# S5 stage: poles turned amid a token tile, six homes for the input tables, stores ahead of loads; last combine: three tiles summed by TensorE

## What is computed

```
A_bar = exp(dt * A);  B_bar = ((A_bar - 1) / A) * B
step: states = scan(A_bar, B_bar u, s);  y = Re(C states)
y = y + d * u
z = gelu(y) @ w_out;  val, gate = split(z);  mix = val * sigmoid(gate)
...
x = layer_norm(ALPHA * x + sum over e of combine[:, e] * (h_e @ w_down[e]))
```

## Time and profile before

| | us |
|---|---|
| median of three runs (1462.12 to 1470.71) | 1466.73 |
| profiled execution | 1460.83 |
| its span, first to last instruction | 1459.3 |
| PE busy / DVE busy / ACT busy in it | 1231.9 / 1005.2 / 708.5 |

### The profile page before, as it was taken

How to read it: one execution, slowest core, us unless ns; L and a number is a source line. 1 busy time by engine, 2 the same in 40 slices (tenths; PEclk the granted TensorE clock), 3 DMA queues, 4 the chain that set the end, 5 groups by cost and what they waited for, 6 DMA issues and landing times.

```text
span 1459.3 us, 17295 instructions
## 1 busy us (share of the span) xinstructions
PE 1231.9 (84%) x6797; PEld 959.3 (66%) x6797; DVE 1005.2 (69%) x1067; ACT 708.5 (49%) x634; POOL 126.0 (9%) x189
## 2 busy tenths in 40 slices
PE   6899998798899999997493834989988999999960
PEld 5898888585466776665372724967854777777740
DVE  5884756445568888787778896342465688888848
ACT  4652332113377777766122813631353777777730
POOL 2000000000400000000300110000004000000021
PEclk9998998598999999999697876999989999999985
DMA  9542010233599999998535053350035999999945
GB/s 266 211 106 74 5 62 6 76 140 116 187 343 383 392 385 382 380 377 298 131 58 102 1 48 19 117 203 31 28 115 196 351 396 396 397 395 380 396 152 148
DMA packets 78929, 301.02 MB, mean 206 GB/s; under 512 B 22965, under 2 KB 40753, under 8 KB 66513
## 3 DMA queue, kind: packets, MB, share of 16 engines
q1 hardware_dynamic: 63128, 246.07, 47.6%
q0 software_dynamic: 15744, 54.18, 11.9%
HBM read 264.23 MB, written 33.64 MB: 204 GB/s over the span
## 4 chain that ended last, share of the span: by engine, by line
PE 57%; DVE 20%; DMA 12%; ACT 6%; issue 3%; SPq 2%; POOL 1%; DVEq 0%; ACTq 0%; POOLq 0%
PE ps L2349 15%; PE ps L2351 14%; PE ps L2350 14%; DMA raw<-in_moe_w_down 7%; DVE wlo L722 4%; ACT whi L629 3%; PE ps L787 2%; DMA u_d<-ub 2%; PE ps L1753 2%; DMA raw<-in_w_in_ab 1%; PE ps L812 1%; PE ps L1751 1%; PE ps L2462 1%; DVE hf L2244 1%; PE ps L2460 1%
## 5 line engine op out<-in xcount | busy, mean ns | idle before, releaser
L722 DVE TENSOR_TENSOR wlo<-raw,whi 128x4096 fp32r<-128x4096 f32 x92 | 406.6, 4422 | 123.6 <-ACT whi L629 123.5
L629 ACT ACTIVATE whi<-raw 128x4096 fp32r<-128x4096 f32 x92 | 333.6, 3628 | 98.4 <-DMA raw<-in_moe_w_down 89.3
L2349 PE MATMUL ps<-whi,xet_lo 128*96 128x512 f32 x528 | 212.6, 403 | 11.4 <-issue 11.2
L2351 PE MATMUL ps<-whi,xet_hi 128*96 128x512 f32 x528 | 208.8, 395 | 0.0
L2350 PE MATMUL ps<-wlo,xet_hi 128*96 128x512 f32 x528 | 208.5, 395 | 0.0
L2349 PE MATMUL ps<-ft_hi,wlo 128*128 128x288 f32 x384 | 120.1, 313 | 3.6 <-DVE wlo L2094 3.6
L2349 PEld LDWEIGHTS ps<-whi,xet_lo 128*96 128x96 f32 x528 | 87.0, 165 | 51.7 <-issue 18.5
L2350 PE MATMUL ps<-ft_lo,whi 128*128 128x288 f32 x384 | 117.1, 305 | 0.0
L2351 PE MATMUL ps<-ft_hi,whi 128*128 128x288 f32 x384 | 116.6, 304 | 0.0
L2351 PEld LDWEIGHTS ps<-whi,xet_hi 128*96 128x96 f32 x528 | 85.7, 162 | 36.8 <-issue 0.2
L2350 PEld LDWEIGHTS ps<-wlo,xet_hi 128*96 128x96 f32 x528 | 86.0, 163 | 34.4 <-issue 1.1
(11 more groups left out here) (455 smaller groups left out, 2110.4 us busy)
## 6 DMA issues: line engine op xcount, KB each, us to landing
raw<-in_moe_w_gate SPq DMA_DIRECT2D x32, 2048.0 KB, 9.6
raw<-in_moe_w_up SPq DMA_DIRECT2D x32, 2048.0 KB, 9.3
raw<-in_moe_w_down SPq DMA_DIRECT2D x32, 2048.0 KB, 9.6
yg<-ysb POOLq DMA_DIRECT2D x32, 384.0 KB, 6.0
xe<-xg POOLq DMA_DIRECT2D x28, 384.0 KB, 8.1
raw<-in_w_in_ab SPq DMA_DIRECT2D x16, 512.0 KB, 6.4
raw<-in_w_out_s SPq DMA_DIRECT2D x4, 2048.0 KB, 8.8
xg<-zeros POOLq DMA_DIRECT2D x4, 1536.0 KB, 14.7
```

What stands on the lines that cost most here:

```text
L629: sa.activation(whi[q][:], raw[q][:], ACT.Copy).then_inc(s(f"hi{q}" + L), 1)
L722: v.tensor_tensor(wlo[q][:], raw[q][:], whi[q][:].bitcast(F32), ALU.subtract).then_inc(s(f"lo{q}" + L), 1)
L2349: te.matmul(out, l_lo, r_hi, start=first, stop=False)
L2351: return te.matmul(out, l_hi, r_hi, start=False, stop=last)
```

## The change

1. `poles_turned`: the seven transposes of the pole tables move from the head of tile 4 to between the two halves of tile 3. ACT's copy to `t4` moves ahead of the copies of tiles 3 and 4.
2. SP's order: the store of tile 0 goes ahead of the loads of B and C, the store of tile 1 and the load of tile 0 between the real and the imaginary part of these, and from then on the store of tile i goes ahead of the load of tile i - 1.
3. Six homes for `wt`: two new ones at `Z_AT`, where the pole tables were. Turns 0 and 1 are made before the wait for the last tile, 2 to 5 after it, 6 and 7 reuse homes 2 and 3 and come after five output turns. `pr` moves to another address and is filled earlier.
4. The output turns run in the order 0, 2, 4, 6, 1, 3, 5, 7, 8, and PE waits for each by its place in it.
5. Last combine, tiles 2 to 4: ACT writes the gates on the diagonals of `dgate`, PE adds `ident` times `xtok` and `dgate` times the two gathered tiles in PSUM, and DVE takes the statistics and the first step of the norm from there.

```diff
+            def u_store(i):
+            def u_load(i):
...
+            u_store(0)
+            sp_.wait_ge(s("ln_x"), 2 * NT)
+            b_and_c(0, "re")
+            u_store(1)
+            u_load(0)
+            b_and_c(1, "im")
+            for i in range(2, NT):
+                u_store(i)
+                u_load(i - 1)
+            u_load(NT - 1)
...
-        wt = [at(f"s5_wt{i}", [P, QT, CL, GC], SPAD_AT + 4 * QT * P * i) for i in range(4)]
+        wt = [at(f"s5_wt{i}", [P, QT, CL, GC], Z_AT + 4 * QT * P * i if i < 2 else SPAD_AT + 4 * QT * P * (i - 2))
+              for i in range(6)]
+        wt += wt[2:4]
...
+        W_PARTS = ((0, 2), (2, 6), (6, 8))
+        O_ORDER = (0, 2, 4, 6, 1, 3, 5, 7, 8)
...
             u_out(2)
+            act.wait_ge(s("s5_pt"), 1)
+            sa.activation(t4[:].rearrange("p a b -> p (a b)"), ps[:, 4, 0:4 * PAIRS], ACT.Copy).then_inc(s("s5a"), 1)
             u_out(3)
+            u_out(4)
             act.wait_ge(s("s5_pt"), 2)
...
+                if t >= 6:
+                    dve.wait_ge(s("s5_fill"), 16 + 2 * (t - 4) + 2)
...
+            w_turns(*W_PARTS[0])
             dve.wait_ge(s("y"), 2 * NT)
...
+            w_turns(*W_PARTS[1])
             dve.wait_ge(s("u72"), 16 * NT)
...
+            o_turns(0, 5)
+            w_turns(*W_PARTS[2])
+            o_turns(5, O_TURNS)
...
+                    if half and poles:
+                        poles_turned()
...
+        def sums_act(act):
+            act.wait_ge(s("routed"), 2)
+            for i in range(SUMMED, NT):
+                n = TILES[i][1]
+                for k in range(2):
+                    ins = nc.scalar.activation(dgate[0:n, i - SUMMED, k, 0:n], ident[0:n, 0:n], ACT.Copy,
+                                               scale=gate[0:n, k, i:i + 1])
+            ins.then_inc(s("x_alpha"), 1)
+        def sums_pe(pe):
+            te = nc.tensor
+            pe.wait_ge(s("x_alpha"), 5)
+            pe.wait_ge(s("got0"), 32 * 3)
+            for i in range(SUMMED, NT):
+                n = TILES[i][1]
+                for half in range(2):
+                    te.matmul(sum_banks(i)[:, half, :], ident[0:n, 0:n], xtok[0:n, i, 512 * half:512 * half + 512],
+                              start=True, stop=False)
+            for i in range(SUMMED, NT):
+                n = TILES[i][1]
+                pe.wait_ge(s(f"got{i % 4}"), 32 * (2 + 2 * (i // 4)))
+                for half in range(2):
+                    for k in range(2):
+                        ins = te.matmul(sum_banks(i)[:, half, :], dgate[0:n, i - SUMMED, k, 0:n],
+                                        ygat[i % 4][k][0:n, 512 * half:512 * half + 512], start=False, stop=(k == 1))
+                ins.then_inc(s("y"), 1)
...
+                if l == 1 and i >= SUMMED:
+                    dve.wait_ge(s("y"), 4 * NT + i - SUMMED + 1)
+                    ln_stats(dve, link, "ffn1", i, sum_banks(i))
+                    ln_norm(dve, link, "ffn1", i, sum_banks(i))
+                    continue
```

More of the change, by code:

```diff
@@ L1075, in s5_sp, with b_and_c @@
                 sp_.dma_start(dst, src).then_inc(s("s5_par"), 16)
[L1076 to L1077 removed]
+            def b_and_c(ri, nm):
                 b_src = a[f"s5_b_{nm}"][0].rearrange("(a b) p c -> (b p) a c", b=2)
@@ L1131, in w_done @@
         def w_done(t):
-            return 12 * (t // 4) + (5, 8, 11, 12)[t % 4]
+            first, last = [part for part in W_PARTS if part[0] <= t < part[1]][0]
+            return 3 * first + (3 * (t - first) + 5 if t < last - 1 else 3 * (last - first))
+        W_PARTS = ((0, 2), (2, 6), (6, 8))
         W_ALL = w_done(7)
         Z_STEPS = NC_P >> LEVELS
+        O_ORDER = (0, 2, 4, 6, 1, 3, 5, 7, 8)
         O_TURNS = 9
@@ L1492, in w_sum, with w_turns @@
             def w_sum(t):
-                dve.wait_ge(s("w_m"), w_done(t) - 3 + (t % 4 == 3) * 2)
-                tt(wt[t % 4][:], wt[t % 4][:], w_tmp[t % 2][:].rearrange("p (a s c) -> p a s c", a=QT, c=GC),
+                dve.wait_ge(s("w_m"), 3 * t + 2)
+                tt(wt[t][:], wt[t][:], w_tmp[t % 2][:].rearrange("p (a s c) -> p a s c", a=QT, c=GC),
                    S_ if t % 2 == 0 else A_).then_inc(s("w_m"), 1)
-            def w_turns(t0, t1, first, last):
-                for t in range(t0, t1):
+            def w_turns(first, last):
+                for t in range(first, last):
                     w_products(t)
@@ L1501, in w_turns @@
                         w_sum(t - 1)
-                if t1 == last:
-                    w_sum(last - 1)
-            w_turns(0, 4, 0, 4)
+                w_sum(last - 1)
+            w_turns(*W_PARTS[0])
+            dve.wait_ge(s("y"), 2 * NT)
+            v.tensor_copy(pf[:], pw[:, :, 0:CL, :])
+            for r_ in range(2):
+                v.tensor_copy(poles[0][:, r_, r_, :], pw[:, 0, CL, :])
+            ts(poles[0][:, 0, 1, :], pw[:, 1, CL, :], -1.0, None, M)
+            v.tensor_copy(poles[0][:, 1, 0, :], pw[:, 1, CL, :]).then_inc(s("bbar"), 1)
+            w_turns(*W_PARTS[1])
             dve.wait_ge(s("u72"), 16 * NT)
@@ L1637, in x_transpose, with token_major @@
                         ins.then_inc(s("xt"), 1)
-            def token_major(i, j, slots, first_chunk, between=None, route=False):
+            def token_major(i, j, slots, first_chunk, between=None, route=False, poles=False):
                 t0, n = TILES[i]
@@ L1672, in s5_pe @@
                 pe.wait_ge(s("x_split"), NT + i + 1)
-                token_major(i, i, (1, 0), 0, 2 * i + 1 if i < 2 else None)
+                token_major(i, i, (1, 0), 0, 2 * i + 1 if i < 2 else None, poles=i == NT - 2)
                 if i < 2:
```

108 lines of the change are left out of this document (55 added, 53 removed).

## The result

The changed kernel takes 1444.9 us (median of 4 runs, 1436.8 to 1450.4) where the kernel before takes 1467.1 us in the runs beside it; the ratio is 0.9851 with a 95% interval of 0.9825 to 0.9878. The forecast was 1444.8 us.

What follows compares the result with a forecast made beforehand. It took SP's store-load DMA chain, with DVE waits beside it, to bound the S5 stage, and DVE the last combine. Gains of 14.0 and 7.9 us, 21.9 in all, from 1466.73 gave 1444.8 us; range 1437 to 1455.

Steps and rivals of the forecast that it cites:

- The powers: S5 stage: with the poles turned amid tile 3, DVE starts the pole powers at 762.0, 8.5 us earlier.
- Stores and loads: S5 stage: SP's new order lands u at 789.7 to 792, before DVE wants it at 795.9; the 1.38 us wait goes.
- cover 4 to 6 us: S5 stage: margin for B and C imaginary, queued behind load 0 on SP, to land before needed; cost nothing.
- rival (e): S5 stage: load 0 and store 1 delay the C loads, DVE and PE wait, kernel slower (1473 at worst landing); chance 0.03.
- Homes and order: S5 stage: DVE's 4.36 us wait for home 0 goes, output tables end at 836.9, not 851.0; stage total 14.0 us.
- The K chain: S5 stage: K starts between 831.3 and 834.7, its 2.94 us wait goes, spreads issue at 850 to 854.3, hidden.
- (b): K chain takes over: PE's clock falls waiting for input turn 6 and stays low into K; 1449 to 1453; chance 0.16.
- 2 to 7: S5 stage: us by which the spreads, landing at 876 to 881, precede the states wanted at 883.1.
- The last combine: Tail: gated sums of tiles 2 to 4 leave DVE, 2.63 us a tile, 7.9 us; PE ahead with 2 us cover.
- Reading PSUM: Last combine: DVE reading PSUM instead of SBUF put at 0, between -0.06 and +0.2 us an instruction.
- The sum and the medians: Whole kernel: 14.0 + 7.9 = 21.9 us, subtracted from the median 1466.73 gives 1444.8; the expert phases shift as a whole.
- rival (a): S5 stage: u comes late, loads landing at 795 to 798, ACT's copies to 801.2; 2.9 us lost, 1447.7; chance 0.10.

Runs made afterwards that it cites:

- e3: Changed kernel with the pole transposes back at the head of the last tile and ACT's copy of them behind the fourth u copy; 1450.5 us, ratio 0.9905.
- e9: Changed kernel with both the poles turned late and SP's old order, keeping six homes, order of turns and new combine; 1455.5 us, ratio 0.9916.
- e4: Changed kernel with SP's old order (B and C ahead of all stores, each load behind its own store); 1447.3 us, ratio 0.9875.
- e10: The changed kernel run once more, without edits; 1448.9 us, ratio 0.9867.
- e5: Changed kernel with the input turns in four homes again, on the weights' slots; 1455.7 us, ratio 0.9911.
- e8: Changed kernel with four tiles summed by TensorE and the identity products ahead of the wait for tile 0's rows; 1447.8 us, ratio 0.9859.
- e11: As e8, with the identity products of tiles 1 to 3 made twice to keep TensorE busy; 1445.0 us, ratio 0.9842.
- e12: Changed kernel, three tiles summed, with the identity products ahead of the wait for tile 0's rows; 1447.3 us, ratio 0.9858.
- after: The changed kernel with all parts of the change, first run; 1444.9 us, ratio 0.9851 to the kernel before.
- e1: Changed kernel with the last combine put back (DVE sums all five tiles), so the S5 part alone; 1452.5 us, ratio 0.9906.
- e7: Changed kernel with four tiles summed by TensorE instead of three; 1450.6 us, ratio 0.9890.
- e6: Changed kernel with the output turns in natural order 0 to 8; 1443.1 us, ratio 0.9816.
- e2: Kernel before with the last combine alone changed (three tiles summed by TensorE); 1458.5 us, ratio 0.9954.
- before: The kernel without the change; 1467.1 us in the runs beside the changed kernel.

## Why the prediction was right

The time, 1444.8, was met, and by its own steps; where a step was off, something next to it absorbed it. That the median came within 0.1 us is luck: the same kernel's second median is 4.0 us higher, and its single executions lie up to 19 us apart. What was right beyond luck is the gain in the traces, 22.05 us for 21.9. Counted from the anchor, predicted times are those of the text less 740.99.

**The powers.** Predicted 8.5 us earlier, measured 8.65 (20.86 for 21.0); the transposes start at 764.18 - 744.29 = 19.89 where 760.9 - 740.99 = 19.9 was read from the middle of tile 3. The attribution was too simple: the 8.5 us were put down to part 1 alone. They are 2.74 by SP's order and then 5.91 by the poles (29.51, 26.77 in e3, 20.86), or in the other order 6.95 by the poles and 1.67 by SP's (29.48 in e9, 22.53 in e4, 20.86).

**Stores and loads.** Here a term was mis-sized. "B and C imaginary to 759" and "cover 4 to 6 us": behind store 1 and load 0 their issue ended at 769.03, 765.7 on the clock of before, and took 11.81 us for eight where 6.93 was taken over from the earlier trace rows. The cover was not 4 us but nothing: in the second trace of the changed kernel (e10) TensorE waits 0.56 us for the last of them in front of its transposes, in e5 to e8, e11 and e12, with the same order there, 0.28 to 0.74 (in after itself and in e1 not at all). ACT's copy of tile 4 comes 38.60 us after the anchor in after and 39.19 in e7, against 38.16 in the kernel before. The tables end at 95.82 to 95.85 in all of these but e5, so it cost nothing. TensorE in e10:

```profile
771.64 1.09 PE L1743 MATMUL ps<-ident,s_craw 128*128 128x128 f32 x8 [0.56 <-DMA s_craw<-in_s_c_im]
```

So rival (e) was nearer than its 0.03 says: with store 1 and load 0 ahead the issue took 5 us longer, and it did push tile 4, by up to 1 us; u had that much to spare. u landed when ACT started its sorting copies, 795.97 - 744.29 = 51.68, which is 792.7 on the clock of before; "789.7 to 792" was 0.7 us short. That it came out free is due to the 795.9 for DVE, which held to 0.2 us (799.06, less 3.30: 795.76).

**Homes and order.** The waits of 4.36 and 1.38 us are gone, output tables predicted at 836.9 and measured at 836.83; 14.0 predicted, 14.17 measured. What the step did not see is the larger half of what the homes do: the wait for the weights' slots that the earlier powers would otherwise have met (5.43 us in e5). The prediction let DVE run from the powers to the sorting copies "without a wait" and was right only because the new homes lie elsewhere.

**The K chain.** Predicted start 831.3 to 834.7, measured 832.24 (835.54 less 3.30); the clock did fall at the wait for input turn 6 (2.12 us where (b) had 3.5), as (b) feared, to 0.57, but was back for K. That it was back is no rule: in e10, the same kernel, K began at 0.50, and in e1, the same S5 stage, it took 17.08 us. The 29 us of (b), all of K at half clock, came in no trace, and the padding of the states stands at 137.36 to 137.44 in all three. Spreads' issue predicted 850 to 854.3, measured 851.55. The DMA engines are busy with them to the window that ends at 882 (its share, 0.96 of 1.5 to 1.7 just before, puts the end near 881.3, 878.0 on the clock of before; 876 to 881 predicted), and the first output product starts at 886.30 behind the padded states, so the cover is some 5 us, inside the "2 to 7". The natural order of output turns makes no difference (e6), where the wait for DVE is gone too; that the order "was made for" the chain was reading a purpose into it.

**The last combine.** 7.9 predicted, 7.88 measured. Inside it, the price of a product was half of what it is: a float32 product shows as two records in the trace (six products are 12 records, a tile's four are 8), and the 0.44 us of the earlier trace rows is that of one record. "Six take 5.3 us at most" is the price at 1.00; they took 7.99 us, since TensorE starts at 0.50 and is back at 1.00 only in the window from 1422. A tile's four take 3.69 us where "1.8 to 3.5" was written. It cost nothing, since the rows came late too (tile 2's at 1424.70). The cover at the last tile is 1.3 us (sums end 1436.81, wanted 1438.09), not 2, and it is thinnest at tile 3: half of the 7.13 us for two tiles puts its sum at 1433.2 (an estimate), wanted at 1433.93.

**Reading PSUM.** The statistics and the first step cost the same from either place (0.69, 0.68, 1.28 us), so the 0 us taken from the earlier trace rows stands. By the Trainium skill's "VectorE: DVE Perf Modes", section on the TRN2 errata, a source in PSUM has 62 cycles more; the nine instructions would have taken 0.6 us more, an estimate from that figure. The trace doesn't agree: none of these instructions is longer from PSUM by more than 0.01 us.

**The sum and the medians.** 21.9 predicted, 22.05 in the landmarks; and "the expert phases shift as a whole" was right in kind, since in no experiment does their length follow the edits, though the pair of profiles alone would have said 13.5 us.

**Two slips without effect.** Of the "five store-load rounds of about 7.4 us" in the earlier trace rows the first takes 3.8 us and only the others 7.4. In rival (a) a landing at 795 to 798 gives copies that end at 798.7 to 801.7, not at 801.2.

## What to carry to other kernels

Where two profiles differ in stretches that nobody edited, count from the nearest untouched instruction ahead of the edit: that gave 0.03 us of agreement here where medians of one kernel differed by 4. The price of a removed wait is what comes next in the engine's list, so edits that remove one wait each are not a sum of parts (the same new buffers were worth 5.5 us alone and 9.5 together with an earlier start). Before work is pulled forward into TensorE's idle time, look at what TensorE does at the end of that time: having finished early it started the critical product at half clock (e8, e12). With three tiles that cost more than finishing late (tail 26.98 us in e12, 26.15 in after). With four it cost less (28.07 in e8, 30.11 in e7), because there the identity products, done late, held up the first sum themselves.

## What the runs showed of the hardware

**Issuing behind a large load.** The issue of the eight C imaginary loads of 32 KB took SP 6.93 us before, and 6.80 to 6.84 us in the three runs with the old order (e2, e4, e9); with a store and a load of u of 480 KB each just ahead of them it took 11.8 to 12.2 us in all ten kernels with the new order. Which of the two holds SP up was not taken apart by an experiment. A hint stands in the same traces: the eight C real loads, behind the store of tile 0 alone, took 7.27 to 7.50 us where they took 6.73 to 6.76 without it. e4, to set beside the row of after:

```profile
752.05 6.81 SPq L1127 DMA_DIRECT2D s_craw<-in_s_c_im  x8
```

**The clock after a short pause.** The first work behind a pause of 5.80 us (e8) and of 12.71 us (e12) ran at 0.50; behind 2.59 us (e11) the windows show 0.62 and 0.52 although the pause itself is at 1.00; the pauses of 0.50 and 1.29 us between the sums in after left it at 1.00. The length of a pause alone doesn't tell what follows. The wait of TensorE in front of K is 2.69 us in every one of these traces: behind it the clock is 1.00 in after, e8, e11 and e12 and falls to 0.50 in before, e1, e6 and e10. So the readings of e8, e11 and e12, one trace each, say what happened there and not what must happen.

**Gathers.** Two gathers of 120 rows of 4 KB are issued every 2.6 us (1.28 us apart on POOL) but land 4.0 to 5.0 us apart (4.03 in e11, 4.47 in e8, 4.98 between tiles 2 and 3 in after), with the DMA share at 1.0 and 217 to 254 GB/s; with the weights' loads the same engines move over 380 GB/s (page of the profile). This pace takes about half of what a fourth summed tile would bring (1.3 of 2.63 us by the estimate for e8); the clock behind the pause took the rest in e11 and more than the rest in e8.

**Weight streaming varies by execution.** From the second gate load to the last down load sixteen experts take 302.4 to 310.6 us in the first layer and 297.7 to 306.4 in the second in fourteen traces of the same code: over 8 us in each, 0.6% of the kernel's time, more than some of the effects under study.
